# Second softmax attention of a two-block transformer kernel: scores and values of two head pairs grouped in each visit of the tiled array

## What is computed

```
q, k = rms_norm_2(q, gq), rms_norm_2(k, gk)
for gi, (window, dilation) in enumerate(((128, 1), (512, 4), (2048, 16))):
    # 8 heads of width 64 in each group
    scores = where(valid, q @ k.T * 64 ** -0.5, -inf)
    p = exp(scores - max); o = p @ v / sum(p)
# head slot i of the three groups is merged by the softmax denominators
gates = sigmoid(p_gate + branch_gate_bias)
mixed = gates[0] * (o_attn @ w_attn_branch) + gates[1] * (o_gla @ w_gla_branch)
x = x + mixed @ w_out
```

## Time and profile before

| | |
|---|---|
| median of 3 runs | 811.54 us |
| span of the profiled execution, first to last instruction | 809.6 us |
| TensorE matmul busy | 804.9 us, 99% |
| VectorE busy | 589.1 us, 73% |
| ScalarE busy | 473.8 us, 59% |
| granted TensorE clock, whole span | 1.000 |
| chain that ended last, TensorE's share | 96% |

### The profile page before, as it was taken

One profiled execution on the slowest core, in us unless ns is written; L12 is line 12 of the kernel. 1 busy time (PEld: TensorE's weight loads), 2 busy tenths in 40 slices (PEclk: granted clock), 3 DMA queues, 4 the chain that ended last, 5 costly groups with the idle time before them and its releaser, 6 DMA issues.

```text
span 809.6 us, 12641 instructions
## 1 busy us (share of the span) xinstructions
PE 804.9 (99%) x4892; PEld 691.3 (85%) x4892; DVE 589.1 (73%) x908; ACT 473.8 (59%) x700; POOL 42.6 (5%) x88
## 2 busy tenths in 40 slices
PE   9999999999999999999999999999999999999998
PEld 8877889888888888888888888999998888888886
DVE  6885799988778788577988863686576855566654
ACT  6876456655656566877565655655844744344442
POOL 0000000000000000003242510100000000000000
PEclk9999999999999999999999999999999999999999
DMA  9953344565555563744454453334355556655551
GB/s 330 351 165 105 105 150 163 188 209 176 192 181 197 197 221 118 275 154 159 160 194 154 169 193 121 105 106 140 128 202 162 185 175 206 208 175 188 172 191 52
DMA packets 90351, 142.08 MB, mean 176 GB/s; under 512 B 3840, under 2 KB 56768, under 8 KB 90176
## 3 DMA queue, kind: packets, MB, share of 16 engines
q1 hardware_dynamic: 89728, 140.38, 51.9%
q10 hardware_dynamic: 576, 1.05, 0.4%
HBM read 140.37 MB, written 1.05 MB: 175 GB/s over the span
## 4 chain that ended last, share of the span: by engine, by line
PE 96%; DVE 2%; DMA 1%; SPq 1%; issue 0%
PE bank L511 21%; PE bank L512 21%; PE bank L513 21%; PE bank L584 16%; PE bank L586 8%; PE bank L382 3%; PE bank L1108 1%; PE bank L1131 1%; DMA vec<-in_vectors 1%; PE bank L1044 1%; DVE w_lo L1782 1%; SPq L413 0%; PE bank L724 0%; PE bank L1068 0%; PE bank L748 0%; PE bank L815 0%
## 5 line engine op out<-in xcount | busy, mean ns | idle before, releaser
L1782 DVE TENSOR_TENSOR w_lo<-raw,w_hi 128x1024 fp32r<-128x1024 f32 (+1 forms) x254 | 302.0, 1215 | 58.4 <-ACT w_hi L1259 57.8
L1259 ACT CAST w_hi<-raw 128x1024 fp32r<-128x1024 f32 (+1 forms) x254 | 260.0, 1045 | 106.7 <-PE bank L513 104.0
L584 PE MATMUL bank<-a_both,w_hi 128*128 128x512 f32 x544 | 193.1, 398 | 0.0
L586 PE MATMUL bank<-a_both,w_lo 128*128 128x256 f32 x544 | 152.7, 281 | 0.0
L511 PE MATMUL bank<-w_hi,h_both 128*128 128x512 f32 (+1 forms) x336 | 133.3, 397 | 0.3 <-DVE w_lo L1782 0.2
L513 PE MATMUL bank<-w_hi,h_both 128*128 128x512 f32 (+1 forms) x336 | 130.4, 388 | 0.0
L512 PE MATMUL bank<-w_lo,h_both 128*128 128x512 f32 (+1 forms) x336 | 130.4, 388 | 0.0
L584 PEld LDWEIGHTS bank<-a_both,w_hi 128*128 128x128 f32 x544 | 102.2, 188 | 25.1
L511 PE MATMUL bank<-w_hi,a_both 128*128 128x512 f32 (+1 forms) x270 | 106.6, 395 | 0.0
L513 PE MATMUL bank<-w_hi,a_both 128*128 128x512 f32 (+1 forms) x270 | 104.9, 389 | 0.0
L512 PE MATMUL bank<-w_lo,a_both 128*128 128x512 f32 (+1 forms) x270 | 104.9, 388 | 0.0
(11 more groups left out here) (234 smaller groups left out, 1038.4 us busy)
## 6 DMA issues: line engine op xcount, KB each, us to landing
raw<-in_w_in SPq DMA_DIRECT2D x45, 1024.0 KB, 5.0
raw<-in_w_up SPq DMA_DIRECT2D x22, 1024.0 KB, 5.0
raw<-in_w_ff_up SPq DMA_DIRECT2D x16, 1024.0 KB, 5.5
raw<-in_w_ff_down SPq DMA_DIRECT2D x16, 1024.0 KB, 4.8
raw<-in_w_down SPq DMA_DIRECT2D x11, 1024.0 KB, 5.0
raw<-in_w_out SPq DMA_DIRECT2D x8, 1024.0 KB, 4.9
raw<-in_w_gla_branch SPq DMA_DIRECT2D x4, 1024.0 KB, 5.0
raw<-in_w_attn_branch SPq DMA_DIRECT2D x2, 1024.0 KB, 4.9
```

What stands on the lines that cost most here:

```text
L584: nc.tensor.matmul(acc.rearrange("p (o t) -> p o t", o=2), w_hi[:, q, k * P:(k + 1) * P], src[:, :, k, :], start=k == 0, stop=False)
L586: ins = nc.tensor.matmul(acc[:, 0:TOKENS], w_lo[:, q, k * P:(k + 1) * P], src[:, 0, k, :], start=False, stop=k == KT - 1)
L1259: nc.scalar.copy(dst, raw_half(m % RAW, half, size, cols)).then_inc(s.hi_done, 1)
L1782: nc.vector.tensor_tensor(dst, raw_half(n // 2 % RAW, n % 2, size, cols), h, ALU.subtract).then_inc(s.lo_done, 1)
```

## The change

The rounds of TensorE are taken two at a time. Four units are turned with 2, 3, 2 and 3 parts behind them; then comes one visit of the tiled array with the scores of the pairs v + 2 and v + 3 and the values of the pairs v and v + 1; then 4 parts. `ppT` gets four places and another spot in SBUF, and `weights_back` waits for the visit two rounds back. VectorE's mask of the next pair stands where it was in even rounds; in odd rounds it moves to the end of the round. All other instructions and their number stay.

```diff
-        ppT = area(10752, 2, 4 * P)
+        ppT = area(12576, 4, 4 * P)
...
-                                               ppT[:, e, b * P:(b + 1) * P], start=b == 0, stop=b == 3)
+                                               ppT[:, 2 * (v % 2) + e, b * P:(b + 1) * P], start=b == 0, stop=b == 3)
...
-            for v in range(AH):
-                att_turn(2 * v)
-                fill(2)
-                att_turn(2 * v + 1)
-                if v + 1 == AH:
+            for v in range(0, AH, 2):
+                for at, parts in enumerate((2, 3, 2)):
+                    att_turn(2 * v + at)
+                    fill(parts)
+                att_turn(2 * v + 3)
+                if v + 2 == AH:
                     pe.wait_ge(s.gla_ready, 1)
                     pe.wait_ge(s.att_masked, 2 * AH)
                     turn_tiles(4, lambda a, k: go[:, a, k * P:(k + 1) * P], s.go_turned, (4, 5))
                 fill(3)
-                if v + 1 == AH:
+                if v + 2 == AH:
                     turn_tiles(4, lambda a, k: go[:, a, 512 + k * P:640 + k * P], s.go_turned, (0, 1))
+                else:
+                    att_score(v + 2)
+                    att_score(v + 3)
                 att_value(v)
-                if v + 2 < AH:
-                    att_score(v + 2)
-                fill(2)
+                att_value(v + 1)
+                fill(4)
...
-                if u >= 2:
-                    act.wait_ge(s.att_pv, u // 2)
-                nc.scalar.copy(ppT[:, u % 2, :], bank[:, 6, :]).then_inc(s.att_pt, 1)
+                if u >= 4:
+                    act.wait_ge(s.att_pv, u // 4 * 2)
+                nc.scalar.copy(ppT[:, u % 4, :], bank[:, 6, :]).then_inc(s.att_pt, 1)
...
+                if v % 2 == 0:
+                    att_mask(v + 1)
                 if v + 1 < AH:
-                    att_mask(v + 1)
                     lo(n + 2 * v)
                 if v < 4:
                     gate_scaled(v)
+                if v % 2 == 1 and v + 1 < AH:
+                    att_mask(v + 1)
```

## The result

The changed kernel takes 819.51 us (median of 4 runs, 818.77 to 820.23), the kernel before 811.56 us on the same chip (4 runs): ratio 1.0096, 95% interval 1.0084 to 1.0108. It is slower by 8 us. The profiled execution is the one of 818.77 us, with a span of 817.0.

What follows compares the result with a forecast made beforehand. TensorE's list was taken to bound the kernel: stalls of 8.7 us less 2.0 saved give 6.7, on the 809.6 us span 816.3, plus 1.9 for the runs' median above the span: 818.2 us, range 815.8 to 820.6.

Steps and rivals of the forecast that it cites:

- What bounds: Attention stage: TensorE never stands still, so its start-to-start distances sum to the time; no new wait is given back downstream.
- The saving: Grouped visits of the tiled array: fewer tiling changes save 0.55 us in each of three, 0.35 in the last; 2.0 us.
- The stalls: TensorE reaches units 2, 6, 10, 14, 15 and 3 before ScalarE and VectorE are done: 8.7 us lost.
- the waits that the prediction named as its signs: TensorE waits for VectorE's scaling four times, about 2.1, 2.1, 1.8 and 1.5 us, and once for ScalarE, about 1 us.
- What costs nothing: Later mask in odd rounds (3 us of cover), four-place `ppT`, its moved area and the later `weights_back` wait: no cost.
- The fourth rival: TensorE's granted clock falls below 1.00; chance 0.05.
- the main case: Whole kernel: stalls of 8.4 to 10.2 us less savings of 1.4 to 2.6, so 817.3 to 820.3 us; chance 0.77.
- The first rival: Grouping alone decides, as the chain to unit 2v + 2 catches up by 2.1 us: 809.5 us; chance 0.06.
- T + 2.60: Even rounds: T starts unit 2v + 1's transposition; TensorE reaches unit 2v + 2 2.60 us later, ready only at T + 4.62.

Runs made afterwards that it cites:

- the run with six parts: Changed kernel with fill parts dealt 2, 6, 2, 1 and 3 behind the visit, instead of 2, 3, 2, 3 and 4: 809.69 us.
- the split visit: The run with six parts, with one part from behind the visit put between its scores and values in three of four double rounds: 810.28 us.
- the run with the old visits: Changed kernel with TensorE's loop of the kernel before (eight visits), all other edits kept: 811.52 us, ratio 1.0001.
- the later ones: Changed kernel measured again, file unchanged: 820.08, 820.07, 820.09 and 821.40 us, at mean clocks of 0.996 to 0.998.
- the run with the hurried lists: Changed kernel with, in even rounds, ScalarE weighing unit 2v + 2 ahead of `hi` and VectorE scaling it ahead of `lo`: 815.94 us.
- all five executions of that kernel: Changed kernel with parts 2, 1, 2, 3 and 6 in the first three double rounds, which lengthens the stalls: 829.28 us, ratio 1.0212.

## Why the prediction was right

**What bounds.** Right: TensorE's list is the time. The stage grew by the stalls less the savings, and no microsecond of it came back later.

**The saving.** Forecast 2.0 us, with values of two pairs at 1.02 + 0.87 = 1.89 us and no row for it. They took 1.90 us, and scores 1.96. The change from scores to values costs what the one behind a fill does, as taken: the run with six parts and the one with the split visit both have 1.90 us for the values. Eleven changes were removed (22 before, 11 after); the run with six parts gained 1.80 us and lost 0.15 at unit 3, so 1.95 / 11 = 0.18 for one, and the split visit measured 0.15 to 0.20.

**The stalls.** Forecast, from the start of the odd turn to the scaled unit against TensorE's own work: 2.07, 2.07, 1.79, 1.47, 1.07 and 0.2, together 8.7 us. From start to start the timeline has 4.68, 4.67, 6.27 and 4.08 us where 4.67, 4.67, 6.27 and 4.07 were forecast, so stalls of 2.08, 2.07, 1.79 and 1.48; unit 15 was stopped for 1.15 and unit 3 for 0.13, together 8.7. Every wait is at the unit and for the engine named. The brackets are 0.15 us shorter than the waits that the prediction named as its signs, since each begins with the end of the last matmul's record. The sum put the restart at zero and kept up to 0.2 us for each stall as an upper end; it is 0.05 us behind a stall, and 0.3 us in all. With it the stage lost 9.0 us (9.1 by the pieces of the chain).

**What costs nothing.** Right by the run with the old visits, and by the absence of any wait in the run with six parts.

**The fourth rival** was given 0.05 and a price of 5.8 us. It took place in part, beside the main case: in two of the four executions on record and in all four of the later ones, at 1.3 to 1.5 us for each time. Its sign, a granted clock under 1.00, did appear. It was wrong to tie it to all four stalls or none. The rule of the Trainium skill that stood beside it (TensorE: Matmul & The Clock Gate, "HAM oscillation") agrees with the traces: the half rate came within or behind idle gaps, with granted clocks of 0.55 and 0.66 in a 5 us stretch. Not every gap of the same length was: of two of 1.9 us in one execution one was followed by it, and none was in the profiled execution of 818.77 us. The two sets of runs can't say why the share differs.

**The number.** 818.2 us was forecast. Executions at full clock took 818.8, 0.6 over: 0.3 for restarts, and 0.3 because the stage began 0.3 us later, ahead of all that the change touches. The median of 819.51 holds 0.7 more, half a clock stretch, as it stands between two executions with one and two without; that it fell there and not at the 820.1 of the later runs is chance.

The first rival (only the grouping counts) gave 809.5 us. It is what the run with six parts measured, 809.7, though not by its condition (unit ready at T + 2.60): the chain is as long as before, and TensorE comes 4.75 us behind the odd turn, when the unit is ready. So the saving was real and the loss was a choice of where to put the fill parts.

## What to carry to other kernels

Where one engine's list is the time and independent work is dealt out between the steps of a chain on other engines, regrouping the steps must keep, between each pair of dependent steps, at least the chain's own length; here 4.67 us were needed and 2.60 were left, while other gaps kept more than they used. Read that length from the timeline before, from the step that releases to the step that waits, with all that stands in the same lists between them. The same 14 parts in another order turned a loss of 8 us into a gain of 1.8.

## What was not expected of the hardware

- A change of tiling costs 0.14 to 0.20 us. Values cost 1.02 us behind scores or behind a fill matmul and 0.88 behind other values (1.90 for two sets); scores 1.08 behind values and 0.88 behind other scores; the first fill matmul behind either 0.32 in place of 0.12.
- TensorE's restart behind a stall costs 0.05 us, whether the stall was 0.21 or 1.93 us long. The chain's 0.66 us in place of 0.44 for the transpositions there holds 0.16 us of the stall, which the bracket leaves out.
- A stall of 1.93 us was followed in some executions by 3.4 us at half clock (fill matmuls every 0.21 us, not 0.12), and not in others of the same kernel; one of 1.96 us in the run with the hurried lists left the clock at 1.000 in all four executions. The stalls of 3.3 to 3.4 us in the profiled execution were followed by it all three times, with TensorE at half rate for 3.4 to 5.6 us, and all five executions of that kernel had a mean clock of 0.992 to 0.994. The fall came between 1.2 us before and 1.1 us after TensorE had begun again. Stalls of 0.5 us and less left the clock at 0.999 to 1.000 in all 11 runs, where it is without them too.
